# A transformer pair with mixture-of-experts layers: early gamma and beta, a second accumulator bank for the last half of the experts, and four more places for expert weights

## The reference, cut to what matters

```python
def grouped_moe(x, router_w, router_bias, w1, w3, w2):
    ...
    gates = jnp.sum(jax.nn.one_hot(idx, N_EXPERTS, dtype=F32) * w[..., None], axis=1)
    h = jax.nn.silu(jnp.einsum('td,edf->etf', xt, w1)) * jnp.einsum('td,edf->etf', xt, w3)
    h = h * gates.T[:, :, None].astype(h.dtype)
    y = jnp.einsum('etf,efd->td', h, w2)

def second_block(...):
    for i in range(DEPTH_2):                        # 2 layers
        ...                                          # i = 0: state space and pooling mixer
        mix = stick_breaking_attention(x @ sb_w_qkv[j]) @ sb_w_out[j]     # i = 1
        x = layer_norm(DEEPNORM_ALPHA * x + mix, ln_mix_g[i], ln_mix_b[i])
        ple = (p[i] @ ple_w_proj[i]) * jax.nn.sigmoid(x @ ple_w_gate[i])
        ffn = grouped_moe(x, router_w, router_bias, moe_w1[i], moe_w3[i], moe_w2[i])
        x = layer_norm(DEEPNORM_ALPHA * x + ffn + ple, ln_ffn_g[i], ln_ffn_b[i])
```

## Time and profile before

| | us |
|---|---|
| median of 3 runs | 1373.17 (1370.04 to 1373.91) |
| the profiled execution, its own time | 1368.77 |
| span of its instructions | 1366.9 |
| TensorE busy | 1279.3 |
| VectorE, ScalarE, GpSimdE busy | 616.9, 470.5, 205.9 |
| mean granted TensorE clock | 0.979 of full |

### The profile page before, as it was taken

The page is one execution under the profiler, slowest core; times in us unless marked ns, Lnnn a source line. Parts: engine busy times, 40 slices in busy tenths (PEclk is TensorE's granted clock), DMA queues, the critical chain, the costliest instruction groups (busy, mean ns, idle before and its releaser), DMA issues.

```text
span 1366.9 us, 18500 instructions
## 1 busy us (share of the span) xinstructions
PE 1279.3 (94%) x7912; PEld 928.4 (68%) x7912; DVE 616.9 (45%) x808; ACT 470.5 (34%) x636; POOL 205.9 (15%) x207
## 2 busy tenths in 40 slices
PE   6999999997999999999899999986999899999994
PEld 6999998875799999888754444424898664444431
DVE  6655556855576665486621111116475651111103
ACT  5544445654345444334411100113576420111101
POOL 0000000500299990030000000000033000000000
PEclk9999999998999999999999999997999999999998
DMA  9555553540455554525669999994423388999994
GB/s 382 187 185 185 185 185 126 194 143 1 162 184 186 185 185 164 185 71 185 241 263 416 421 421 422 421 421 184 174 101 124 123 302 319 423 421 421 421 421 163
DMA packets 47750, 338.33 MB, mean 248 GB/s; under 512 B 5296, under 2 KB 5296, under 8 KB 7728
## 3 DMA queue, kind: packets, MB, share of 16 engines
q1 hardware_dynamic: 45936, 330.53, 63.1%
q10 hardware_dynamic: 1728, 6.55, 1.3%
HBM read 336.02 MB, written 1.05 MB: 247 GB/s over the span
## 4 chain that ended last, share of the span: by engine, by line
PE 83%; DVE 8%; DMA 5%; ACT 2%; issue 1%; SPq 0%; ACTq 0%; DVEq 0%
PE pb L177 82%; DMA ring<-in_moe_w 3%; DVE halves L295 1%; DMA XN<-in_ln_b 1%; ACT halves L287 1%; DMA ring<-in_ffn_w 1%; DVE SM L1439 1%; DVE Xs L1450 1%; PE pb L1876 0%; DVE Xs L387 0%; DVE Xs L389 0%; DVE XN L326 0%; DVE Xs L1445 0%; DVE slots_y L2009 0%; ACT slots_y L1978 0%
## 5 line engine op out<-in xcount | busy, mean ns | idle before, releaser
L295 DVE TENSOR_TENSOR halves<-ring,halves 128x2048 fp32r<-128x2048 f32 (+1 forms) x122 | 285.4, 2354 | 151.0 <-ACT halves L287 150.9
L177 PE MATMUL pb<-XTh,halves 128*128 128x256 f32 x1856 | 338.8, 283 | 7.1 <-DVE XTl L376 5.2
L177 PEld LDWEIGHTS pb<-XTh,halves 128*128 128x128 f32 x1856 | 291.2, 192 | 9.4 <-issue 4.1
L177 PE MATMUL pb<-XTl,halves 128*128 128x256 f32 x928 | 262.4, 283 | 0.0
L287 ACT CAST halves<-ring 128x2048 fp32r<-128x2048 f32 (+1 forms) x122 | 227.3, 1874 | 94.1 <-PE pb L177 90.2
L177 PE MATMUL pb<-ring,gather 128*64 128x512 f32 x1024 | 233.4, 598 | 4.4 <-DVE gather L2005 1.7
L177 PEld LDWEIGHTS pb<-XTl,halves 128*128 128x128 f32 x928 | 177.8, 192 | 0.9
L177 PE MATMUL pb<-halves,XTh 128*128 128x512 f32 x512 | 160.4, 394 | 6.1 <-DVE halves L295 3.1
L177 PEld LDWEIGHTS pb<-ring,gather 128*64 128x64 f32 x1024 | 71.1, 137 | 135.3 <-issue 131.0
L177 PE MATMUL pb<-ring,slots_ht 128*64 128x512 f32 x512 | 116.8, 598 | 3.3 <-DMA ring<-in_moe_w 2.4
L2001 DVE TENSOR_TENSOR slots_h<-slots_silu,pb 128x256 f32<-128x256 f32 x32 | 13.5, 421 | 230.7 <-ACT slots_silu L1966 230.7
(11 more groups left out here) (343 smaller groups left out, 1281.2 us busy)
## 6 DMA issues: line engine op xcount, KB each, us to landing
ring<-in_moe_w SPq DMA_DIRECT2D x192, 1024.0 KB, 13.4
ring<-in_ffn_w SPq DMA_DIRECT2D x66, 1024.0 KB, 4.9
ring<-in_w_tok SPq DMA_DIRECT2D x10, 1024.0 KB, 5.0
ring<-in_ple_gate SPq DMA_DIRECT2D x8, 1024.0 KB, 4.9
ring<-in_w_out SPq DMA_DIRECT2D x4, 1024.0 KB, 4.9
ring<-in_ab_out SPq DMA_DIRECT2D x4, 1024.0 KB, 4.9
ring<-in_sb_v SPq DMA_DIRECT2D x4, 1024.0 KB, 23.6
ring<-in_sb_q SPq DMA_DIRECT2D x4, 1024.0 KB, 12.4
```

The source lines that it names most:

```text
L177: return e.matmul(out, l, r, start=start, stop=stop, **kw)
L295: e.tensor_tensor(l, raw_of(n), h.bitcast(F32), ALU.subtract).then_inc(*low.mark(n))
```

## The change

It has four parts.

1. `EXTRA = 4` places more for the blocks of the experts. Two are `XTh` and `XTl`, free once the last `ple_gate` block has been used; two lie in `rest`, and the DMAs that first fill them wait for `ple_added(i, 2)` besides.
2. `down_bank`: the last `down` (pair 7, second half) writes bank 5 and not 4. It waits for `mul(7, 0)`, the last reader of bank 5, and no longer for `y_low(7, 0)`. `spread(7, 0)` now stands behind that `down`, directly ahead of `spread(7, 1)`.
3. `act_norm_load` for the norm after the experts is issued by ScalarE in step 7 of 8, after `gathered(7, 1)`, the last read of `XN`.
4. Ahead of the attention, x tile 0 is turned as soon as it is normed, and two of the idle matmuls stand between the tiles, on bank 0, with no wait of their own; before, both tiles stood behind them, and they waited for the variance of tile 1.

The dense branch is adapted to it: it takes x from 16 transposes of its own, has its gamma and beta early too, and other addresses. The attention itself is the same on both sides.

```diff
@@ -18,6 +18,7 @@
...
 SPLIT = 4
+EXTRA = 4
 SCOLS = 2048
@@ -245,10 +246,17 @@
...
 
-        home, high_home, gone, high_gone, landed = [], [], [], [], []
-        latest, landings = [-1] * (RING + SPLIT), [0] * (RING + SPLIT)
+        home, high_home, gone, high_gone, landed, after_ple = [], [], [], [], [], {}
+        latest, landings = [-1] * (RING + SPLIT + EXTRA), [0] * (RING + SPLIT + EXTRA)
         for n in range(len(plan)):
-            at = min(range(RING + SPLIT if n in whole else RING), key=lambda s: latest[s])
+            if n in whole and n - 1 not in whole:
+                latest[RING + SPLIT:] = [n - 1] * EXTRA
+                fresh = {RING + SPLIT + 2, RING + SPLIT + 3}
+            at = min(range(RING + SPLIT + EXTRA if n in whole else RING), key=lambda s: latest[s])
+            if n in whole and at in fresh:
+                fresh.remove(at)
+                after_ple[n] = max(i for i in range(2) if index[("moe", i), "w13", 0, 0, 0] <= n)
             home.append(at)
@@ -260,10 +268,14 @@
...
 
-        land = [sem(f"land{i}") for i in range(RING + SPLIT)]
+        land = [sem(f"land{i}") for i in range(RING + SPLIT + EXTRA)]
         high, low, used = signal("w_high"), signal("w_low"), signal("w_used")
 
+        extra = [place(f"extra{i}", at, SCOLS) for i, at in enumerate((xt_at, xt_at + 2048, rest, rest + 4096))]
         def place_of(x, s, n):
+            if s >= RING + SPLIT:
+                return extra[s - RING - SPLIT][:, 0:plan[n].shape[-1]]
             return x[:, s * SCOLS:s * SCOLS + plan[n].shape[-1]]
@@ -310,6 +322,8 @@
...
                     e.wait_ge(*used.at(gone[n]))
+                if n in after_ple:
+                    e.wait_ge(*ple_added.at(after_ple[n], 2))
                 e.dma_start(raw_of(n), src).then_inc(land[home[n]], 16)
@@ -340,8 +354,10 @@
...
 
-        def pe_turn(e, key, src3, ready):
+        def pe_turn(e, key, src3, ready, between=None):
             for t in range(2):
+                if t and between:
+                    between()
                 e.wait_ge(*ready(t))
@@ -1842,6 +1858,9 @@
...
 
+        def down_bank(p, h):
+            return banks[5 if p == 7 and h else 4]
@@ -1877,9 +1896,11 @@
...
             def down(p, h):
-                D = banks[4]
-                if h:
+                D = down_bank(p, h)
+                if h and p < 7:
                     e.wait_ge(*s.y_low.at(p, 0))
+                elif h:
+                    e.wait_ge(*s.mul.at(7, 0))
                 else:
@@ -1940,7 +1961,7 @@
...
                         spread(p - 2, 1)
-                    if n == 1 and p >= 1:
+                    if n == 1 and 1 <= p < 8:
                         spread(p - 1, 0)
@@ -1954,6 +1975,7 @@
...
                         down(p - 1, n)
+            spread(7, 0)
             spread(7, 1)
@@ -1975,7 +1997,7 @@
...
                     e.wait_ge(*s.gate_kept.at())
-                e.activation(Y[h][0], banks[4][:, :], ACT.Copy, scale=slot_gate[:, p:p + 1]).then_inc(*s.y_high.mark(p, h))
+                e.activation(Y[h][0], down_bank(p, h)[:, :], ACT.Copy, scale=slot_gate[:, p:p + 1]).then_inc(*s.y_high.mark(p, h))
 
@@ -1990,6 +2012,9 @@
...
                         high(p - 1, n)
+                if p == 7:
+                    e.wait_ge(*s.gathered.at(7, 1))
+                    act_norm_load(e, 2 * i + 1)
 
@@ -2006,7 +2031,7 @@
...
                 e.wait_ge(*s.y_high.at(p, h))
-                e.scalar_tensor_tensor(Y[h][1], banks[4][:, :], slot_gate[:, p:p + 1], Y[h][0].bitcast(F32), ALU.mult,
+                e.scalar_tensor_tensor(Y[h][1], down_bank(p, h)[:, :], slot_gate[:, p:p + 1], Y[h][0].bitcast(F32), ALU.mult,
                                        ALU.subtract).then_inc(*s.y_low.mark(p, h))
...
@@ -2154,9 +2190,9 @@
...
         def pe_program(e, c):
-            def idle(n):
+            def idle(n, P=banks[7]):
                 for _ in range(n):
-                    mm(e, banks[7][:, :], ident, CO[:, 0:512], True, True)
+                    mm(e, P[:, :], ident, CO[:, 0:512], True, True)
 
@@ -2178,9 +2214,7 @@
...
                     idle(3)
-                    e.wait_ge(*variance.at(1, 1))
-                    idle(2)
-                    pe_turn(e, "stick", X3, normed_x(1))
+                    pe_turn(e, "stick", X3, normed_x(1), lambda: idle(2, banks[0]))
                     pe_stick(e)
@@ -2230,8 +2264,6 @@
...
                     act_dense(e, c, dense[i])
-                e.wait_ge(moe_half[i], 1)
-                act_norm_load(e, 2 * i + 1)
                 act_norm(e, 2 * i + 1)
```

More of the change, by code:

```diff
@@ L2031, in dve_slots @@
                         low(p - 1, n)
-        GG, gT = place("dense_gates", rest, 4096), place("dense_gate_t", rest + 4096, 256)
-        HTD = [[place(f"dense_ht{p}{x}", rest + 4608 + 2048 * p + 1024 * x, 1024).rearrange("p (c t) -> p c t", c=4)
+        GG, gT = place("dense_gates", rest + 10496, 4096), place("dense_gate_t", rest + 14848, 256)
+        HTD = [[place(f"dense_ht{p}{x}", rest + 6144 + 2048 * p + 1024 * x, 1024).rearrange("p (c t) -> p c t", c=4)
                 for x in range(2)] for p in range(2)]
-        SD = [place(f"dense_silu{x}", rest + 8704 + 512 * x, 512) for x in range(2)]
-        XD = place("dense_x", xt_at, 2048)
+        SD = [place(f"dense_silu{x}", rest + 15104 + 512 * x, 512) for x in range(2)]
+        XD = place("dense_x", rest + 2048, 2048)
         XD3 = XD.rearrange("p (k t) -> p k t", k=8)
@@ L2045, in __init__ @@
                 pe, act, dve = line(f"d{i}_pe"), line(f"d{i}_act"), line(f"d{i}_dve")
-                self.turned, self.rows = signal("turned", pe), signal("rows", pe)
+                self.x_turned, self.turned, self.rows = signal("x_turned", pe), signal("turned", pe), signal("rows", pe)
                 self.gates, self.silu = signal("gates", act), signal("silu", act)
@@ L2079, in pe_dense @@
             e.wait_ge(*ple_added.at(i, 2))
+            for kp in range(4):
+                for k in range(2):
+                    for t in range(2):
+                        j = e.transpose(banks[kp][:, k * 256 + t * 128:k * 256 + t * 128 + 128],
+                                        XN3[:, t, (2 * kp + k) * 128:(2 * kp + k + 1) * 128], ident)
+            j.then_inc(*f.x_turned.mark())
             for t in range(2):
@@ L2104, in act_dense @@
         def act_dense(e, c, f):
+            e.wait_ge(*f.x_turned.at())
+            act_norm_load(e, 2 * f.i + 1)
             e.wait_ge(*ple_added.at(f.i, 2))
@@ L2122, in dve_dense @@
             e.tensor_copy(gT[0:16, :], banks[4][0:16, 0:256]).then_inc(*f.kept.mark())
-            e.tensor_tensor(XD, XTh.bitcast(F32), XTl.bitcast(F32), ALU.add).then_inc(*f.whole.mark())
+            e.wait_ge(*f.x_turned.at())
+            for kp in range(4):
+                j = e.tensor_copy(XD[:, kp * 512:kp * 512 + 512], banks[kp][:, :])
+            j.then_inc(*f.whole.mark())
             for p in range(8):
```

## The result

The changed kernel takes 1353.94 us (median of 4 runs, 1351.21 to 1357.50), against 1372.57 us (1370.04 to 1373.91, 4 runs) before: a ratio of 0.9868, 95% interval 0.9844 to 0.9893. The profiled execution took 1351.21 us, with a span of 1349.4 us and a mean clock of 0.981, against 1368.77 and 1366.9 us before.

The account below looks back on a forecast made before the run. TensorE was taken to bound the kernel nearly everywhere. Savings of 11.0 us in layer 0 and 5.1 in layer 1, together 16.1, gave 1357.1 us against the median of 1373.17, range 1352 to 1363.

Parts of the forecast that it names:

- What bounds the kernel: In the experts, TensorE sets the pace nearly everywhere, 13.93 us per half of a pair, though the DMAs are full.
- Part 1: Extra places in the experts save only TensorE's waits for blocks: 1.1 us in layer 0, 2.4 in layer 1.
- all four are worth their DMA time: Rival in the experts: DMAs bound the layer, places give 9.9 us a layer, 16.3 us more, 1341; chance 0.03.
- Part 2: At the end of each layer's experts, the second bank saves 2.7 us, 5.4 in all; between 1.4 and 3.7.
- D + 10.13: First add of bank 1, counted from the start of down(7, 0), expected 10.13 us later; before, 12.86.
- Part 3: In the norm after the experts, early gamma and beta save 7.2 us in layer 0 and nothing in layer 1.
- The rival of late loads: Layer 0's norm: beta lands behind the ring at 924.6 or 927.1, losing 1.3 to 3.8 us, up to 1361; chance 0.11.
- the bound used (909.6): Latest time, in us, for ScalarE's issue of beta in layer 0, so that beta is there by 922.4.
- The other estimate: Gamma and beta from ScalarE's queue, taking turns with the ring: through in some 5 us, 1 MB at half rate.
- Part 4: The turn ahead of the attention costs between 0 and 1.1 us; 0 was taken.
- The sum: Whole kernel: 11.0 us in layer 0 and 5.1 in layer 1, 16.1 together; 1352.7 profiled, 1357.1 against the median.
- Slower: Rival: the attention's projections start at the low clock and stay there, costing 22 us, 1379; chance 0.03.

Follow-up runs that it names:

- e1: The changed kernel with EXTRA = 0, so no extra places for expert blocks: 1360.51 us, ratio 0.9931 to the kernel before.
- e7: The kernel before with only the early gamma and beta loads added: 1365.51 us over 10 runs, ratio 0.9948 to the kernel before.
- e2: The changed kernel with EXTRA = 2, the places of the turned x alone: 1355.29 us, ratio 0.9883 to the kernel before.
- e3: The changed kernel with the last down back in bank 4 and spread(7, 0) back between the two down: 1359.24 us, ratio 0.9928 to the kernel before.
- e4: The changed kernel with gamma and beta loaded late again, after moe_half: 1361.34 us, ratio 0.9937 to the kernel before.
- e5: The changed kernel with the old order of idle matmuls and turning ahead of the attention: 1354.36 us, ratio 0.9859 to the kernel before.
- e6: The changed kernel without the five idle matmuls ahead of the attention: 1356.03 us, ratio 0.9878 to the kernel before.
- e8: The changed kernel with two ScalarE splits (not four), one VectorE split (not two) ahead of the turned x, three idle matmuls (not five): 1352.36 us, ratio 0.9847.
- e9: The changed kernel itself, measured again: 1355.02 us over 6 runs, ratio 0.9873 to the kernel before.
- e10: The kernel of e8 again, on the same chip as e9: 1348.56 us over 5 runs, ratio 0.9825 to the kernel before.

## Why the prediction came out right

**What bounds the kernel.** Right. The half of a pair stayed at 13.93 us with the DMAs at 0.98, and with no places at all (e1) the loss was the waits and no more.

**Part 1.** Forecast 1.1 + 2.4 = 3.5 us, the wait table's sum. The stretches to D0 and D1 give 1.28 + 2.93 = 4.2, with one fall of the clock in each on both sides. The term was 0.7 us too small: the wait table was taken for the whole of it, but a wait counts there only from the modelled end of the row before. At 0.17 us for each of three waits (e1) that is 0.5 of the 0.7; the other 0.2 stays open. The same loss differs between executions: up to D0 and D1, against runs with places and the same clock, it was 1.3 and 2.9 us before, 3.1 and 1.8 in e1, 1.7 and 2.4 in e7. In e1, 0.5 us a layer are lost behind D0 and D1, where before's order had no wait: the second bank makes its two `down` want their blocks closer together, a dependence between parts 1 and 2 that the prediction didn't have. That all four are worth their DMA time was rightly left out; e2 shows that two would do. The forecast did not ask how many are needed.

**Part 2.** Forecast 2.7 us a layer, measured 2.94 and 2.97 here and 2.95 in e3. The sum was D + 10.13, and it came at D + 9.92: it took two `down` at 3.65 us each, 7.30, and as one row of 32 they take 7.09, which is the whole difference. The adds did end level with the chain (920.70 against the last spread's end at 920.75), so their lost cover cost nothing.

**Part 3.** Forecast 7.2 and 0 us, measured 7.20 and 0. e7 gives the same with nothing else changed. The rival of late loads fell: beta was issued at 907.85, 1.75 us ahead of the bound used (909.6), landed at 919.3 and was wanted at 924.5. The other estimate, 5 us for both loads by turns between the queues, was too low: it took a turn for half of the bytes, and here it is a third (last section). What the forecast did not say is that the parts overlap: with the other three in place, the late loads would have cost 4.6 us and not 7.2 (e4), because the ring that has run ahead leaves the DMAs partly idle behind the experts (0.56 where it was 0.96).

**Part 4.** Forecast 0 (0 to 1.1 us), measured 0: 8.93 us from the variance to the first projection in the kernels before, after, e5 and e6. The forecast had ScalarE's four splits as what the turn must not outlast, and chose 0 because TensorE would be done in time. e6 and e8 bear this out. What it did not draw from it is that part 4 could then bring nothing, and that fewer splits would bring 3.1 us.

**The sum.** 16.1 us from before's own 1368.77 made 1352.7; the profiled execution took 1351.21. By terms: part 1 +0.7, part 2 +0.5, part 3 0, part 4 0, which makes 17.3; the clock in the projections gave 1.63 that no step had, and the layers ahead of the change cost 1.42: 17.5. So that the total of the profile came within 1.5 us is in part luck: two terms outside the mechanism nearly cancel. Against the medians, 18.6 us are between 1372.57 and 1353.94, and the forecast of 1357.1 lies 3.2 above. Of these 0.6 is the median of before, which a fourth run moved from 1373.17 to 1372.57, and the rest is the larger gain.

**Slower.** The projections began at the high level in the profile after (0.70 us for the first pair) and at the low one in e6, where it lasted into their first 5 us, and took 33.5 to 35.9 us in all eleven profiles since. The 22 us of the slow rival did not come near.

## What to carry to other kernels

When the DMA share is 1.0 and the computing engine's pace is unbroken, price more buffers at that engine's waits, not at the DMA time that they fill, and ask how few will do; an entry of the wait table is a lower bound where rows overlap. Where a chain of engines sets a stretch (here 8.93 us), moving the engine that waits last changes nothing; take work away ahead of the ones that release it. Parts that shorten the same wait do not add: 7.2 us alone were 4.6 beside the others.

## What the runs showed of the hardware

**The same instructions differ by some 9 us.** T0, ahead of everything that the change touches, lay between 689.1 us (e3) and 698.1 us (e2). Two places of it in e2, in the chain and by stretch, to be set beside `318.30 7.10 PE pb L178 x46` and the first stretch of the profile after, where the clock at 582 to 588 is 1.00:

```profile
316.02 12.09 PE pb L178 x46
```

```profile
318.00:324.00 6.00, 6.00 (x22) 3.45 (x21) 1.05 (x4) 2.55 (x14) 0.00 (x0) 0.50 0.00 0
582.00:588.00 6.00, 6.00 (x130) 6.00 (x125) 0.00 (x0) 0.00 (x0) 0.00 (x0) 0.54 0.20 79
```

A granted clock of 0.50 is 1.2 GHz. The same 46 rows took 7.10, 8.59, 11.85 or 12.09 us over the twelve profiles. So a comparison of 1% is better made by stretches between the same events than by spans.

**Steps of 1.6 us are short falls of the clock.** T0 to D0, with no wait for a block, took 218.5 us where the granted clock stayed at 1.00 (e2, e4, e5, e6, e9), 220.1 where it fell to 0.50 once for some 3.4 us (after, e10), and 221.8 where it lay there twice as long (e3, e8). Here is the place, 12.5 us behind T0, in the profile after and in e9, the same kernel:

```profile
703.20:706.40 3.20, 3.20 (x16) 3.20 (x16) 0.33 (x2) 0.00 (x0) 0.00 (x0) 0.50 1.00 415
```

```profile
709.13:712.33 3.20, 3.20 (x26) 2.51 (x27) 1.02 (x3) 0.00 (x0) 0.00 (x0) 1.00 1.00 420
```

From T0 (690.72) to 703.20 TensorE was busy 12.48 of 12.48 us, so no pause of it lies in that time ahead of the fall. The projections' long value is the same fall (before, e1, e3, e7), the short one has none (after, e2, e5, e8, e9, e10), and in e4 and e6 the clock was low when they began. All six short ones are kernels with parts 1, 2 and 3, and the four long ones and e4 each lack one of these. So this fall may go with how the layer ahead ends; with one profile of most kernels that is not shown, and what makes the clock fall stays open in all of them.

**A load on a second queue beside a full ring.** Half a block of beta took 11.4 us from issue to landing after layer 0, and gamma 8.0; after layer 1, where the ring has nothing left to bring, 4.9 and 3.5. The Trainium skill, page "DMA: Bandwidth & Descriptors", section "Queues, rings and completion order", has each engine take turns between its queues, a packet from each, from which the prediction estimated 5 us for both, at half of the rate. The trace agrees with the turns, and not with the half. Between 911 and 919 us (SyncE's queue is q1, ScalarE's q10: packets, MB, share of the engines' time):

```profile
q1 hardware_dynamic: 315, 2.29, 68.6%
q10 hardware_dynamic: 286, 1.04, 32.6%
```

286 packets against 315 are nearly one each. But one of the ring carries a row of 8 KB and one of gamma or beta a row of 4 KB, so ScalarE's queue gets a third of the bytes, and its 1 MB takes some 8 us. The other 3 us lie ahead of the turns: gamma was issued at 907.47, and only 2 packets of q10 moved before 911. What holds them there stays open.
